# Grouped attention: outputs one pair of units later, shares copied by VectorE

## Chip, cores and metric

One NeuronCore of a Trainium2 chip runs the whole program. The metric is the device time in microseconds of one execution, as the median of several runs. All engines run at once and are held together by semaphores that the program waits on. TensorE multiplies, VectorE and ScalarE work on rows, GpSimd does a little arithmetic and issues transfers, SyncE issues the stream of weights.

## What is computed

The reference is a two-layer block, then a second block with grouped attention, retention and a mixture of experts. The change touches only the grouped attention of the second block:

```python
def one_block(q_blk):        # 128 queries; 8 query heads, 2 key/value heads, 64 features each
    s = jnp.einsum('bqhgd,bkhd->bhgqk', q_blk, k).astype(jnp.float32) * scale
    p = jax.nn.softmax(s, axis=-1)
    return jnp.einsum('bhgqk,bkhd->bqhgd', p.astype(v.dtype), v)
```

There are 512 queries (`LT` = 4 tiles of 128) and 768 keys (`NT` = 6 tiles of 128: 256 of the context and 512 latent). So there are 4 x 8 = 32 units (`S_UNITS`), each one query tile of one head, with 128 x 768 scores.

## The kernel before

**Units and pairs.** Units are done in pairs u, u+1 (u even). The two units of a pair belong to the two key/value heads, and lie in the two halves of the partitions for the scores' inputs and for the outputs. A unit goes through four jobs: scores `S` (three passes of products, high and low parts, 128 x 768), row maximum and exponential, transposes `T` of the six 128 x 128 pieces, and outputs `O`.

**PSUM slots.** PSUM is cut into four slots of two banks (1024 float32 columns). A job takes a slot: `begin` waits until the job before it in that slot was evacuated (`s_ev`), `end` tells that it is filled (`s_mm`). `filled` and `evacuated` are the waits for these, `own(...)` issues an instruction and has its engine wait for its end, `own.free(...)` issues it without. The slots and the order of all jobs are written by `make_plan`; `attention_jobs` gives the grouped attention's: `S` of unit n in slot n % 2, `T` and `O` of unit n in slot 2 + n % 2. TensorE walks the jobs in exactly this order.

**TensorE per pair (lines 2386 to 2405).** Transposes of u, transposes of u+1, scores of u+2 and u+3, then a job `O` u with the shares and a job `O` u+1 with the outputs. The shares: VectorE writes `share`, the identity scaled by the reciprocal sum of each row; a product with ones turns it into a PSUM tile in which each column holds the reciprocal of its query, laid out as the transposed outputs are. After u = 24 comes the modulation product `ada(2, 8)` in slot 2, after the loop `ada(2, 9)`, then the retention products (line 2427).

**ScalarE per pair (lines 1121 to 1138).** Copies of both units' transposes from PSUM into `ptg`; `out_high` of the pair before (the high part of `o_f` into `xth`); copy of the shares from PSUM into `shares`; exponentials of u+2 and u+3 (line 1005), which also sum the rows and free the scores' slots. After u = 6 it makes the exponential of `near`, the powers of the retention decay.

**VectorE per pair (lines 1760 to 1782).** Row maxima of u+2 and u+3 (line 1512); `out_low` of the pair before (line 1754); the outputs times `shares` into `o_f` (line 1769), which frees the outputs' slot; `sharing(u + 2)`, the reciprocal and two scaled identities (lines 1743, 1747); then a piece of other work: in pairs 4 to 7 two low parts of weights (line 1228), from pair 8 two sums of a modulation chunk (line 1275; the first of a chunk is line 1273). In pair 1 it writes `near` (lines 1562 to 1565), after pair 12 it adds the bias of `ada(2, 8)` (line 1288).

**SyncE** streams the weights through three buffers `raw` (line 628). The second half of modulation chunk 9 goes into the buffer that chunk 8 leaves, so its transfer waits for the product `ada(2, 8)`; VectorE needs it at its first sum of pair 14.

Of the kernel before, what the change touches and what calls it, by code (L numbers as in the profile page):

```python
# [16 lines left out]
P = 128  # L17
# [105 lines left out]
def make_plan(src):  # L123
# [123 lines left out]
    attention_jobs(plan, "gqa", range(S_UNITS), (24, lambda: plan.job("ada", 2, 8, slot=2)))  # L247
# [30 lines left out]
def build(nc, src, out):  # L278
# [8 lines left out]
    with ExitStack() as stack:  # L287
# [17 lines left out]
        sb("gate_region", [P, 2 * KB])  # L305

# [99 lines left out]
        sin_t = sb("sin_t", [P, SEQ])  # L406
        vecs = sb("vecs", [P, VECS])
# [3 lines left out]
        tmp = sb("tmp", [P, 2, TOK])  # L411
# [426 lines left out]
        def _(act):  # L838
# [275 lines left out]
            def out_high(u):  # L1114

                m, h = gqa_unit(u)
                evacuated(act, "O", "gqa", u + 1)
# [99 lines left out]
        def _(dve):  # L1217
# [339 lines left out]
            def near_powers():  # L1557

                d = dist[:, R_ZERO:R_ZERO + P]
                back = tmp[:, 1, 0:R_HEADS * P].rearrange("p (h n) -> p h n", h=R_HEADS)  # L1560
                for h in range(R_HEADS):
                    own.free(nc.vector.tensor_scalar(near[:, h, :], d, 0.0, lg[:, h:h + 1], ALU.max, ALU.mult))
                    own.free(nc.vector.tensor_scalar(back[:, h, :], d, 0.0, lgt[:, h:h + 1], ALU.min, ALU.mult))
                own.wait()
                own(nc.vector.tensor_tensor(near[:], near[:], back, ALU.add), s_arg)
# [172 lines left out]
            def sharing(u):  # L1738
# [5 lines left out]
                if u >= 2:  # L1744
                    filled(dve, "O", "gqa", u - 2)
                for n in range(2):
                    own.free(nc.vector.tensor_scalar(share[:, n, :], ident[:], st[:, n, 3:4], None, ALU.mult), s_share)

            def out_low(u):
# [5 lines left out]
                                                 ALU.subtract), s_ol)  # L1755

# [3 lines left out]
            for i in range(S_UNITS // 2):  # L1760
# [979 lines left out]
```

## Time and profile before

| | |
|---|---|
| runs shown (3) | median 1795.95 us, 1794.54 to 1797.14 |
| the profiled execution | 1800.47 us, its span 1798.8 us |
| busy over the span | TensorE 88%, VectorE 51%, ScalarE 30%, GpSimd 10% |
| grouped attention | 1012 to 1112.75 us |
| chain that ended last | TensorE 56%, transfers 16%, VectorE 16%, ScalarE 4% |

The profile is of one execution, by its hardware records. The busy windows give each engine's busy time and TensorE's granted clock in a stretch (1.00 is 2.4 GHz, 0.50 is 1.2 GHz). The chain of waits goes back from the last instruction to what released each one. The timeline lists instructions in order of time, equal ones merged. "Issue" is time in which an engine waited for nothing that the profile shows. Matmuls are pipelined, so a group's busy time overlaps its neighbours'.

### The profile page before, as it was taken

What the parts mean: (1) busy time and instruction counts of PE and PEld (TensorE: products, weight loads), DVE (VectorE), ACT (ScalarE), POOL (GpSimd) and SP (SyncE); (2) the same over time, 40 slices, a digit from 0 to 9 for tenths busy, and PEclk for the clock granted to TensorE, in tenths of its full rate; (3) what the DMA queues carried; (4) which work ended last, traced back from release to release, by engine and by line L of the source; (5) the groups of instructions that cost most, each with busy time, mean ns of one, the idle gap of its engine ahead of it and who ended that gap; (6) DMA issues with size and microseconds to landing.
All of it is one profiled execution on the core that took longest, in us unless ns stands there. A gap on an engine that the chain in (4) does not pass through costs nothing.

```text
span 1798.8 us, 22831 instructions
## 1 busy us (share of the span) xinstructions
PE 1587.1 (88%) x8464; PEld 1131.5 (63%) x8464; DVE 911.0 (51%) x1578; ACT 539.1 (30%) x859; POOL 181.2 (10%) x263
## 2 busy tenths in 40 slices
PE   6699999799799989998999888796999898989880
PEld 6588888688688868787788677676434333333330
DVE  3876537567458656576597876764121111111115
ACT  3312222467233354443523475122111110101011
POOL 2000010023110100001201300110000000000002
PEclk9899999769899999999999899895999999999995
DMA  9232354100332310223444012226999999999984
GB/s 371 73 115 94 137 192 169 53 13 20 115 126 89 136 49 36 105 72 140 160 177 150 1 48 95 103 90 250 366 423 423 423 423 422 423 423 423 423 355 146
DMA packets 55795, 353.07 MB, mean 196 GB/s; under 512 B 7408, under 2 KB 7664, under 8 KB 18720
## 3 DMA queue, kind: packets, MB, share of 16 engines
q1 hardware_dynamic: 43056, 306.88, 42.6%
q0 software_dynamic: 12656, 45.07, 6.8%
q8 instruction: 53, 0.87, 0.2%
q14 instruction: 30, 0.25, 0.0%
HBM read 332.26 MB, written 23.59 MB: 198 GB/s over the span
## 4 chain that ended last, share of the span: by engine, by line
PE 56%; DMA 16%; DVE 16%; ACT 4%; issue 3%; SPq 3%; POOL 0%; DVEq 0%; POOLq 0%; ACTq 0%
PE ps L2081 10%; DMA early<-in_experts 10%; PE ps L2083 10%; PE ps L2082 10%; PE ps L2563 6%; PE ps L2135 3%; DMA raw<-in_experts 3%; PE ps L2584 3%; PE ps L2267 3%; SPq L640 2%; PE ps L2544 2%; PE ps L2291 2%; PE ps L2060 1%; PE ps L2284 1%; DMA early<-in_ada 1%
## 5 line engine op out<-in xcount | busy, mean ns | idle before, releaser
L2081 PE MATMUL ps<-whi,xth 128*128 128x512 f32 (+1 forms) x768 | 305.7, 398 | 12.6 <-DVE xtl L1623 5.4
L2082 PE MATMUL ps<-wlo,xth 128*128 128x512 f32 (+1 forms) x768 | 302.0, 393 | 0.0
L2083 PE MATMUL ps<-whi,xtl 128*128 128x512 f32 (+1 forms) x768 | 301.6, 393 | 0.0
L1981 DVE TENSOR_TENSOR hid<-hid,ps 128x256 f32<-128x256 f32 x33 | 13.9, 422 | 370.4 <-ACT hid L1179 370.4
L2081 PEld LDWEIGHTS ps<-whi,xth 128*128 128x128 f32 x768 | 148.4, 193 | 43.0 <-DVE xtl L1623 5.7
L2083 PEld LDWEIGHTS ps<-whi,xtl 128*128 128x128 f32 x768 | 148.0, 193 | 30.3
L2082 PEld LDWEIGHTS ps<-wlo,xth 128*128 128x128 f32 x768 | 148.5, 193 | 28.9
L2563 PE MATMUL ps<-early,xe_t 128*64 128x512 f32 x624 | 142.3, 596 | 13.9 <-DMA early<-in_experts 12.9
L1228 DVE TENSOR_TENSOR wlo<-raw,whi 128x2048 fp32r<-128x2048 f32 (+3 forms) x52 | 103.1, 1984 | 70.6 <-ACT whi L850 64.4
L850 ACT ACTIVATE whi<-raw 128x2048 fp32r<-128x2048 f32 (+2 forms) x46 | 85.5, 1858 | 123.1 <-DMA raw<-in_even 33.5
L2563 PE MATMUL ps<-raw,xe_t 128*64 128x512 f32 x432 | 101.1, 600 | 19.1 <-DMA raw<-in_experts 16.1
L2563 PEld LDWEIGHTS ps<-early,xe_t 128*64 128x64 f32 x624 | 43.1, 137 | 109.4 <-issue 74.1
L1275 DVE SCALAR_TENSOR_TENSOR raw<-raw,cvec 128x512 f32<-128x512 f32 x140 | 105.2, 752 | 4.8
L2584 PE MATMUL ps<-early,hid_t 128*64 128x512 f32 x408 | 94.9, 601 | 1.7 <-DVE hid_t L1985 0.5
L1512 DVE TENSOR_REDUCE stat<-ps 128x1 f32<-128x768 f32 x64 | 61.3, 957 | 62.1 <-PE ps L2284 50.3
L1179 ACT ACTIVATE hid<-ps 128x256 f32<-128x256 f32 x33 | 12.7, 384 | 253.9 <-PE ps L2563 253.9
L2563 PEld LDWEIGHTS ps<-raw,xe_t 128*64 128x64 f32 x432 | 28.1, 136 | 89.2 <-issue 45.1
L818 POOL DMA_DIRECT2D pair_dram<-tmp x66 | 34.5, 523 | 471.3 <-ACT tmp L1184 468.2
L2544 PE MATMUL ps<-h2h,hot 128*128 128x512 f32 x144 | 61.2, 425 | 6.1 <-DVE hot L1969 6.1
L667 POOL TENSOR_SCALAR stat<-stat 128x1 f32<-128x1 f32 (+3 forms) x36 | 12.0, 334 | 533.5 <-ACT xtl_f L949 156.7
L1184 ACT ACTIVATE tmp<-ps 128x512 f32<-128x512 f32 x33 | 19.7, 597 | 136.8 <-PE ps L2584 136.8
L2584 PEld LDWEIGHTS ps<-early,hid_t 128*64 128x64 f32 x408 | 26.4, 136 | 51.0 <-issue 45.5
(438 smaller groups left out, 2829.5 us busy)
## 6 DMA issues: line engine op xcount, KB each, us to landing
early<-in_experts SPq DMA_DIRECT2D x129, 1024.0 KB, 26.1
raw<-in_experts SPq DMA_DIRECT2D x54, 1024.0 KB, 26.1
raw<-in_ada SPq DMA_DIRECT2D x40, 1024.0 KB, 6.6
ring<-in_experts SPq DMA_DIRECT2D x15, 1024.0 KB, 27.7
raw<-in_even SPq DMA_DIRECT2D x14, 1024.0 KB, 5.2
raw<-in_second SPq DMA_DIRECT2D x10, 1024.0 KB, 5.4
pair_dram<-tmp POOLq DMA_DIRECT2D x66, 128.0 KB, 5.8
early<-in_ada SPq DMA_DIRECT2D x8, 1024.0 KB, 18.4
```

Of the source, the lines that this page charges most:

```text
L850: own(nc.scalar.activation(whi[:, k % SPLIT, 0:w], raw[:, number[splits[k]["name"]] % RAW, 0:w], ACT.Copy), s_hi)
L1228: own(nc.vector.tensor_tensor(wlo[:, k % SPLIT, at_], raw[:, g % RAW, at_], whi[:, k % SPLIT, at_].bitcast(F32), ALU.subtract), s_lo if pa ...
L1275: ins = nc.vector.scalar_tensor_tensor(dst, w[kt // 4][:, kt % 4, :], cv, dst, ALU.mult, ALU.add)
L1512: own(nc.vector.tensor_reduce(st[:, 1:2], v[:, 0:TOK], AX, ALU.max, negate=True), nb)
L2081: nc.tensor.matmul(v, a[0], b[0], start=first, stop=False)
L2082: nc.tensor.matmul(v, a[0], b[1], start=False, stop=False)
L2083: return nc.tensor.matmul(v, a[1], b[0], start=False, stop=last)
L2135: mm = nc.tensor.transpose(v[:, to:to + P], rows_, ident[:])
L2267: mm = nc.tensor.matmul(v[:, TOK:TOK + n], pts[w % 2][:, P * a:P * a + P], v_of(w, a), start=a == 0, stop=a == NT - 1)
L2544: mm = nc.tensor.matmul(ps[:, h, :], hot[:, m, :], part[:, m, 512 * h:512 * h + 512], start=m == 0 and part is h2h, stop=m == LT - 1 and p ...
L2563: mm = nc.tensor.matmul(ps[SLOT * t:SLOT * t + SLOT, 4 + s, :], xe_t[:, 2 * i + k, SLOT * s:SLOT * s + SLOT], w[:, D * k + 512 * t:D * k + ...
L2584: mm = nc.tensor.matmul(ps[SLOT * t:SLOT * t + SLOT, 7, :], hid_t[:, s, P * c + SLOT * k:P * c + SLOT * k + SLOT], w[:, D * k + 512 * t:D ...
```

## The change

- **Order.** TensorE runs T(u), S(u+2) and S(u+3), O(u-2), T(u+1). The outputs of a pair come one pair later, between the scores of the next pair and the transposes of the second unit. The last outputs follow the loop.
- **One job for the outputs.** Shares and outputs of a pair are one job `O` u in slot 2 (columns 896 to 1023 and 768 to 895). `T` of even units stays in slot 2, of odd ones in slot 3.
- **Shares by VectorE.** `out_shared` copies the shares from PSUM into `r_f` on VectorE, waits for itself, and multiplies. ScalarE's copy is gone. `out_high` and `out_low` run two pairs late instead of one. In VectorE's round `sharing` now stands after the weights' parts.
- **Buffers.** `ptg` and `share` are doubled; the second `ptg` is `tmp`. `near` moves into free halves of `cos_t` and `sin_t`, in two pieces, so its exponential is two instructions.
- **Modulation chunk 8.** Its product comes after u = 26 instead of 24, in slot 3 instead of 2; VectorE adds its bias in pair 13 instead of 12.

```diff
--- before.py
+++ after.py
@@ make_plan
-    attention_jobs(plan, "gqa", range(S_UNITS), (24, lambda: plan.job("ada", 2, 8, slot=2)))
+    for u in range(2):
+        plan.job("S", "gqa", u, slot=u)
+    for u in range(0, S_UNITS + 2, 2):
+        if u < S_UNITS:
+            plan.job("T", "gqa", u, slot=2)
+            for n in (u + 2, u + 3):
+                if n < S_UNITS:
+                    plan.job("S", "gqa", n, slot=n % 2)
+            if u:
+                plan.job("O", "gqa", u - 2, slot=2)
+            plan.job("T", "gqa", u + 1, slot=3)
+        else:
+            plan.job("O", "gqa", u - 2, slot=2)
+        if u == 26:
+            plan.job("ada", 2, 8, slot=3)
+    plan.next = 0
...
@@ buffers
-        near = at("near", xt_base, 20 * KB, [P, R_HEADS, P])
-        share = at("share", xt_base, 45 * KB, [P, 2, P])
-        shares = at("shares", xt_base, 46 * KB, [P, 2, P])
-        ptg = at("ptg", g_base, 0, [P, 2, TOK])
+        share = at("share", xt_base, 45 * KB, [P, 2, 2, P])
+        r_f = at("r_f", xt_base, 21 * KB, [P, P])
+        ptg = [at("ptg0", g_base, 0, [P, 2, TOK]), tmp]
+        near = [t[:, SEQ // 2:SEQ].rearrange("p (h n) -> p h n", h=2) for t in (cos_t, sin_t)]
...
@@ ScalarE
+            def keys_first(n):
+                v = filled(act, "T", "gqa", n)
+                if n >= 4:
+                    filled(act, "O", "gqa", n // 2 * 2 - 4)
+                own.free(nc.scalar.activation(ptg[n // 2 % 2][:, n % 2, :], v[:, 0:TOK], ACT.Copy), ev("T", "gqa", n))
+
             for u in range(0, S_UNITS, 2):
-                for n in (u, u + 1):
-                    v = filled(act, "T", "gqa", n)
-                    if u >= 2:
-                        filled(act, "O", "gqa", u - 1)
-                    own.free(nc.scalar.activation(ptg[:, n % 2, :], v[:, 0:TOK], ACT.Copy), ev("T", "gqa", n))
-                if u >= 2:
-                    out_high(u - 2)
-                v = filled(act, "O", "gqa", u)
+                keys_first(u)
                 if u >= 4:
-                    evacuated(act, "O", "gqa", u - 3)
-                own.free(nc.scalar.activation(shares[:, u // 2 % 2, :], v[:, TOK:TOK + P], ACT.Copy), ev("O", "gqa", u))
+                    out_high(u - 4)
                 if u + 2 < S_UNITS:
                     exps("gqa", u + 2, pg, s_nbg)
                     exps("gqa", u + 3, pg, s_nbg)
+                keys_first(u + 1)
                 if u == 6:
                     act.wait_ge(s_arg, 3)
-                    own.free(nc.scalar.activation(near[:], near[:], ACT.Exp), s_fade)
+                    for j in range(2):
+                        own.free(nc.scalar.activation(near[j], near[j], ACT.Exp), s_fade)
+            out_high(S_UNITS - 4)
             out_high(S_UNITS - 2)
...
@@ VectorE
-                if u >= 2:
-                    filled(dve, "O", "gqa", u - 2)
+                if u >= 4:
+                    filled(dve, "O", "gqa", u - 4)
...
+            def out_shared(u):
+
+                v = filled(dve, "O", "gqa", u)
+                own(nc.vector.tensor_copy(r_f[:], v[:, TOK + P:TOK + 2 * P]))
+                own(nc.vector.tensor_tensor(o_f[:, u // 2 % 2, :], v[:, TOK:TOK + P], r_f[:], ALU.mult), ev("O", "gqa", u))
...
                 if i:
-                    out_low(u - 2)
-                v = filled(dve, "O", "gqa", u + 1)
-                evacuated(dve, "O", "gqa", u)
-                own(nc.vector.tensor_tensor(o_f[:, i % 2, :], v[:, TOK:TOK + P], shares[:, i % 2, :], ALU.mult),
-                    ev("O", "gqa", u + 1))
-                if u + 2 < S_UNITS:
-                    sharing(u + 2)
+                    out_shared(u - 2)
+                if i >= 2:
+                    out_low(u - 4)
                 if 4 <= i < 8:
                     for n in range(2):
                         low_part(("sout", "o", (i - 4) // 2), 2 * (i % 2) + n, 4)
                 elif i >= 8:
                     for n in range(2):
                         add_part(2, 8 + (i - 8) // 4, 2 * (i % 4) + n)
+                if u + 2 < S_UNITS:
+                    sharing(u + 2)
                 if i == 1:
                     near_powers()
-                if i == 12:
+                if i == 13:
                     ada(2, 8)
+            out_low(S_UNITS - 4)
+            out_shared(S_UNITS - 2)
             out_low(S_UNITS - 2)
...
@@ TensorE
+            def gqa_turn(w):
+                evacuated(pe, "S", "gqa", w)
+                turn(("T", "gqa", w), [pg[:, w % 3, P * a:P * a + P] for a in range(NT)], [P * a for a in range(NT)])
+
+            def gqa_out(u):
                 v = begin("O", "gqa", u)
                 pe.wait_ge(s_share, u + 2)
...
+                evacuated(pe, "T", "gqa", u + 1)
                 for a in range(NT):
...
+            gqa_scores(0)
+            for u in range(0, S_UNITS, 2):
+                gqa_turn(u)
+                if u + 2 < S_UNITS:
+                    gqa_scores(u + 2)
+                if u:
+                    gqa_out(u - 2)
+                gqa_turn(u + 1)
+                if u == 26:
                     ada(2, 8)
+            gqa_out(S_UNITS - 2)
```

## Rows read from the trace of the kernel before

**Rows 1.** Busy windows: the stretch, its length, each engine's busy time, clock, transfers

```profile
core 0: us, PE busy (x) PEld busy (x) DVE busy (x) ACT busy (x) POOL busy (x), PEclk, DMA share, GB/s
...
1066.00:1071.30 5.30, 4.66 (x53) 3.78 (x52) 4.33 (x10) 4.05 (x8) 0.00 (x0) 1.00 0.57 184
...
1095.60:1101.80 6.20, 6.08 (x53) 4.98 (x52) 3.05 (x8) 4.17 (x9) 0.00 (x0) 0.73 0.39 161
...
1012.00:1112.75 100.75, 81.97 (x846) 66.93 (x845) 74.18 (x147) 65.03 (x129) 15.61 (x8) 0.92 0.12 43
...
1112.75:1115.75 3.00, 3.00 (x29) 3.00 (x30) 0.16 (x1) 0.00 (x0) 0.00 (x0) 0.50 0.54 175
```

**Rows 2.** Chain of waits, one steady pair: start, duration, engine and what it wrote

```profile
1066.06 1.27 PE ps L2381 x11
...
1068.47 0.95 ACT pg L1005 x2
1069.53 0.73 issue
```

**Rows 3.** Chain of waits: the row maxima that begin pairs 2, 12, 13 and 14

```profile
1035.64 0.97 DVE stat L1512
...
1088.76 0.97 DVE stat L1512
...
1097.96 0.97 DVE stat L1512
...
1103.30 0.97 DVE stat L1512
```

**Rows 4.** Timeline around the modulation product of chunk 8: start, duration, instruction, wait

```profile
1090.24 1.05 PE L2060 MATMUL ps<-half,raw 128*128 128x1 f32 x8
...
1093.83 0.16 DVE L1288 TENSOR_TENSOR mod<-ps,vecs 128x4 f32<-128x4 f32 x1
1094.11 1.29 PEld L2135 LDWEIGHTS ps<-ident,pg 128*128 128x128 f32 x12 [2.90 <-issue]
```

**Rows 5.** Timeline at the stage's end: the modulation product of chunk 9

```profile
1111.74 1.08 PE L2060 MATMUL ps<-half,raw 128*128 128x1 f32 x8 [2.06 <-DVE raw L1275]
```

**Rows 6.** Waits of the transfer queue from 1205 us: total, times, longest

```profile
SPq L640 <- PE ps L2563: 59.8, 12, 48.1
```

**Rows 7.** Timeline of one steady pair: TensorE, and ScalarE's copy of transposes

```profile
1065.18 0.87 PE L2135 MATMUL ps<-ident,pg 128*128 128x128 f32 x6
1065.99 0.50 PE L2381 MATMUL ps<-ka_h,qa_h 64*128 64x512 f32 x2
...
1067.51 1.48 PE L2401 MATMUL ps<-ptg,kk 128*64 128x128 f32 x24
...
1066.10 0.81 ACT L1126 ACTIVATE ptg<-ps 128x768 f32<-128x768 f32 x1 [0.18 <-PE ps L2135]
```

**Rows 8.** Timeline of one steady pair: VectorE

```profile
1065.26 0.17 DVE L1743 RECIPROCAL stat<-stat 128x2 f32<-128x2 f32 x1 [0.69 <-ACT pg L1005]
...
1065.86 1.41 DVE L1228 TENSOR_TENSOR wlo<-raw,whi 128x512 fp32r<-128x512 f32 x2
1067.42 1.95 DVE L1512 TENSOR_REDUCE stat<-ps 128x1 f32<-128x768 f32 x2
1069.41 0.29 DVE L1754 TENSOR_TENSOR xtl<-o_f,xth 128x128 fp32r<-128x128 f32 x1
1069.62 0.28 DVE L1769 TENSOR_TENSOR o_f<-ps,shares 128x128 f32<-128x128 f32 x1
```

**Rows 9.** VectorE's copies from PSUM elsewhere: shortest/median/longest ns, first and last start

```profile
L1985 DVE COPY hid_t<-ps x33: 423/425/425, 1269.1 to 1749.8; 128x256 f32<-128x256 f32 x33
...
L1975 DVE COPY xe_t<-ps x36: 680/691/693, 1258.0 to 1740.4; 128x512 f32<-128x512 f32 x36
```

**Rows 10.** Timeline: two modulation sums on VectorE in one pair

```profile
1081.85 1.53 DVE L1275 SCALAR_TENSOR_TENSOR raw<-raw,cvec 128x512 f32<-128x512 f32 x2
```

**Rows 11.** Timeline: the exponential of the powers on ScalarE

```profile
1043.83 0.62 ACT L1138 ACTIVATE near<-near 128x512 f32<-128x512 f32 x1
```

**Rows 12.** Timeline at the stage's start: VectorE's first shares, GpSimd's products

```profile
1016.72 6.50 DVE L1747 TENSOR_SCALAR share<-ident,stat 128x128 f32<-128x128 f32 x2
...
1018.61 4.52 POOL L789 TENSOR_TENSOR gr_b<-gr,gn 128x2048 f32<-128x2048 f32 x1
```

**Rows 13.** Transfer issues from 1090.5 to 1091.6: size, us from issue to landing

```profile
raw<-in_ada SPq DMA_DIRECT2D x1, 1024.0 KB, 4.9
```

More of the change, by code:

```diff
@@ L305, in build @@
         sb("gate_region", [P, 2 * KB])
+        tmp = sb("tmp", [P, 2, TOK])
         def at(name, base, offset, shape, dt=F32):
@@ L369, in build @@
         rk_t = at("rk_t", xt_base, 12 * KB, [P, 2, 2, SEQ])
-        near = at("near", xt_base, 20 * KB, [P, R_HEADS, P])
+        near_back = at("near_back", xt_base, 20 * KB, [P, 2, P])
         pg = at("pg", xt_base, 36 * KB, [P, 3, TOK])
-        share = at("share", xt_base, 45 * KB, [P, 2, P])
-        shares = at("shares", xt_base, 46 * KB, [P, 2, P])
+        share = at("share", xt_base, 45 * KB, [P, 2, 2, P])
         o_f = at("o_f", xt_base, 47 * KB, [P, 2, P])
-        ptg = at("ptg", g_base, 0, [P, 2, TOK])
+        r_f = at("r_f", xt_base, 21 * KB, [P, P])
+        ptg = [at("ptg0", g_base, 0, [P, 2, TOK]), tmp]
         qw_t = at("qw_t", xt_base, 36 * KB, [P, R_HEADS, SEQ])
@@ L1559, in near_powers @@
                 d = dist[:, R_ZERO:R_ZERO + P]
[L1560 to L1565, printed above, removed]
+                for j in range(2):
+                    for i in range(2):
+                        h = 2 * j + i
+                        own.free(nc.vector.tensor_scalar(near[j][:, i, :], d, 0.0, lg[:, h:h + 1], ALU.max, ALU.mult))
+                        own.free(nc.vector.tensor_scalar(near_back[:, i, :], d, 0.0, lgt[:, h:h + 1], ALU.min, ALU.mult))
+                    own.wait()
+                    own(nc.vector.tensor_tensor(near[j], near[j], near_back[:], ALU.add), s_arg if j else None)
             for i in range(2):
@@ L1743, in sharing @@
                 own(nc.vector.reciprocal(st[:, :, 3:4], st[:, :, 2:3]))
-                if u >= 2:
-                    filled(dve, "O", "gqa", u - 2)
+                if u >= 4:
+                    filled(dve, "O", "gqa", u - 4)
                 for n in range(2):
-                    own.free(nc.vector.tensor_scalar(share[:, n, :], ident[:], st[:, n, 3:4], None, ALU.mult), s_share)
+                    own.free(nc.vector.tensor_scalar(share[:, u // 2 % 2, n, :], ident[:], st[:, n, 3:4], None, ALU.mult), s_share)
             def out_low(u):
@@ L1802, in states @@
                     if n == 1:
-                        dve.wait_ge(s_fade, 3)
+                        dve.wait_ge(s_fade, 4)
                         weighted_scores(0)
@@ L1810, in weighted_scores @@
                 two = slice(2 * j, 2 * j + 2)
-                own.free(nc.vector.tensor_tensor(sw[:, two], v, near[:, two, :].unsqueeze(2).broadcast_to([P, 2, LT, P]),
+                own.free(nc.vector.tensor_tensor(sw[:, two], v, near[j].unsqueeze(2).broadcast_to([P, 2, LT, P]),
                                                  ALU.mult), ev("RS", j))
@@ L2383, in gqa_scores @@
                                 end(mm, "S", "gqa", u + i)
-            gqa_scores(0)
-            for u in range(0, S_UNITS, 2):
-                for w in (u, u + 1):
-                    evacuated(pe, "S", "gqa", w)
-                    turn(("T", "gqa", w), [pg[:, w % 3, P * a:P * a + P] for a in range(NT)], [P * a for a in range(NT)])
-                if u + 2 < S_UNITS:
-                    gqa_scores(u + 2)
+            def gqa_turn(w):
+                evacuated(pe, "S", "gqa", w)
+                turn(("T", "gqa", w), [pg[:, w % 3, P * a:P * a + P] for a in range(NT)], [P * a for a in range(NT)])
+            def gqa_out(u):
                 v = begin("O", "gqa", u)
@@ L2394, in _ @@
                 for i in range(2):
-                    mm = nc.tensor.matmul(v[halves[i], TOK:TOK + P], half[:, 1:2].broadcast_to([P, 64]), share[:, i, :],
-                                          start=True, stop=True)
-                end(mm, "O", "gqa", u)
-                v = begin("O", "gqa", u + 1)
+                    nc.tensor.matmul(v[halves[i], TOK + P:TOK + 2 * P], half[:, 1:2].broadcast_to([P, 64]),
+                                     share[:, u // 2 % 2, i, :], start=True, stop=True)
+                evacuated(pe, "T", "gqa", u + 1)
                 for a in range(NT):
@@ L2401, in _ @@
                         mm = nc.tensor.matmul(v[halves[i], TOK:TOK + P], kk[:, a, P + 64 * i:P + 64 * i + 64],
-                                              ptg[:, i, P * a:P * a + P], start=a == 0, stop=a == NT - 1)
-                end(mm, "O", "gqa", u + 1)
-                if u == 24:
+                                              ptg[u // 2 % 2][:, i, P * a:P * a + P], start=a == 0, stop=a == NT - 1)
+                end(mm, "O", "gqa", u)
+            gqa_scores(0)
[7 more added lines that the diff above has]
+                if u == 26:
                     ada(2, 8)
+            gqa_out(S_UNITS - 2)
             ada(2, 9)
```

3 lines of the change are left out of this document (1 added, 2 removed).

## The prediction

> **What bounds the kernel now.** I read the busy windows first, the chain of waits next, then the timeline of one pair of units. The windows show that in the grouped attention (1012 to 1112.75 us, 100.75 us) no engine is full: TensorE 82.0 us, VectorE 74.2, ScalarE 65.0, granted clock 0.92 [rows 1]. A stage like that is set by a loop of waits. The chain of one steady pair names it: scores on TensorE, the row maximum on VectorE, the exponential on ScalarE, 0.73 us of "issue" (the second unit's exponential), then the second unit's transposes, which stand ahead of the next scores [rows 2]. Its length is the distance of the row maxima: from 1035.64 to 1088.76 there are ten pairs, 5.31 us each; in the piece used below, 5.33 [rows 3]. The next pair takes 9.20 us (1088.76 to 1097.96), because the modulation product of chunk 8 stands there, the one after 5.34, and from 1103.30 to the start of the retention products (1112.82) it is 9.52 [rows 3, 4, 5].
>
> What follows the stage is timed by its start: TensorE, ScalarE and VectorE in turn until the experts, and there the transfer queue has waited 48.1 us for TensorE [rows 6]. A microsecond won here should reach the end.
>
> **The steady pair after the change.** M is the start of the first row maximum of a pair. TensorE now runs T(u), scores of u+2 and u+3, outputs of u-2, T(u+1). The scores wait for exp(u+1) and T(u), no longer for T(u+1): 0.87 us of transposes and their hand-over leave the old loop, 5.33 - 0.9 = 4.4 us [rows 7]. But the outputs of u-2 now lie in the slot that T(u+2) needs, and they come free only when VectorE has done both maxima and then copied and multiplied. So a new loop is late next:
> - two maxima 1.95, hand-over 0.03 [rows 8]
> - the new copy 128x128 from PSUM: copies from PSUM took 0.425 at 256 columns and 0.691 at 512 [rows 9], on a line 0.29 at 128. Bounds: 0.17, the reciprocal of two columns, and 0.425. I take 0.29.
> - wait for itself 0.04, product 0.28 [rows 8], hand-over to TensorE 0.12 (from the modulation's end to the next transposes, 1093.99 to 1094.11 [rows 4])
> - T(u+2) 0.81 until the scores issue, scores 1.33 to their end, 0.10 to the maximum [rows 2, 7, 8].
>
> Sum 4.95 us. VectorE's own round is the third loop: 1.98 for the maxima, 0.33 copy, 0.32 product, 0.25 for the low part, then reciprocal, shares and two weight parts 2.05 (1065.26 to 1067.27 and 0.04), which is 4.93; with two modulation sums of 1.53 instead of 1.41 it is 5.05 [rows 8, 10]. Removing ScalarE's copy of the shares (0.28) earns nothing by itself: ScalarE waits for the maximum anyway. TensorE's issue per pair is 1.62 for transposes, 1.26 scores, 1.75 outputs, some 4.5, below all of these. The outputs of u-2 need the slot's transposes copied by ScalarE: two exponentials, then two copies of 0.81 [rows 7], end 4.65 us after M, 0.1 us before TensorE wants them: covered, but barely. If that cover goes, the delay goes straight into the pair.
>
> Six of the ten pairs go by 4.95, four by some 5.03 (the first sum of a chunk is cheaper): 49.8 instead of 53.1, a gain of 3.3. Once ScalarE makes the powers' exponential (0.62 before, two pieces now, some 0.75) between maxima and copies that are now on the edge [rows 11]; I charge 0.4. **Steady part: -2.9.** With the copy at its bounds it is -4.2 (VectorE's round then limits the last pairs) or -1.4.
>
> **The start.** The first shares take 6.50 us because VectorE sits behind GpSimd's product that ends at 1023.1 [rows 12]. The change leaves that order alone, so max(2) starts at about 1023.1 in both. Then T(2) need not wait for the first outputs, but TensorE has stood idle 2 us longer and issues it and the scores at 1.2 GHz; the powers on VectorE follow later in its round. I get max(6) at 1035.2 instead of 1035.64: **-0.4**, bounds 0 and -2.
>
> **The modulation product.** Before, chunk 8 shares slot 2 with the next transposes: they wait for TensorE's 1.05 us product and for VectorE, which first does shares and two sums (1093.83) [rows 4]. After, it comes after T(27) in slot 3, while T(28) uses slot 2. The pair from M(26) to M(28) becomes an ordinary one, 5.03 instead of 9.20: **-4.2**. The next pays: the product waits until ScalarE has copied T(27), which stands behind exp(28) and exp(29). T(27) is done 3.7 us after the scores of 28 begin, the copy 5.3, the product runs to 6.4, T(28) to 7.2, scores and hand-over 1.43: M(30) is 7.2 after M(28) instead of 5.34: **+1.9**. Before, the clock fell in this place, 0.73 over the next pair [rows 1], and the scores took 0.95 longer. The idle time is 1.5 us now against 2.8; I charge half of it: **+0.5**.
>
> The half chunk of weights that the queue loads behind this product is needed by VectorE at its sum in pair 14. Before, a whole pair lay between; now 5.2 us. It landed in 4.9 [rows 13]: no wait, with 0.2 to spare. Bounds 0 and 2 us.
>
> **The end.** Without scores the last outputs are strung out: O(28) needs T(30) copied, O(30) needs O(28) multiplied and T(31) copied, and only then comes the product of chunk 9. From M(30): out_shared(26) ends 2.6, T(30) 3.5, its copy 4.7, O(28) 6.5, T(31) 7.3, its copy 8.1, O(30) 9.5, product 10.6, against 9.5 before, where the product waited 2.06 for VectorE's sums [rows 5]: **+1.1**.
>
> **Sum:** -2.9 - 0.4 - 4.2 + 1.9 + 0.5 + 1.1 = -4.0 us. The profiled execution was 1800.47 (span 1798.8 and 1.7 around it), so 1796.5; the shown runs have the median 1795.95, 4.5 lower, so 1791.9. What can be told from no change here is about 0.2%, 3.6 us: the forecast lies just beyond it.
>
> **Rivals.**
> (a) VectorE takes the steady gain back. For: it is at 4.3 of 5.3 us in a pair [rows 1], and the loop now runs through it twice over. If copy and hand-overs cost 0.4 more per pair, the steady part is near 0 and the whole -1.1: 1794.8. Against: its rows are regular to 0.01 us. Chance 0.22, within 0.2%.
> (b) The clock holds. After chunk 9 the retention products ran 3.0 us at 0.50, TensorE having waited 2.06 just before [rows 1, 5]; now it waits less there. At 2.4 GHz they save 1.5, and the 0.5 charged above goes: 1789.9. Chance 0.2, faster.
> (c) The clock falls, the other side. Transposes, scores and outputs are now separated by waits on two engines, and one fall costs more since TensorE's 4.5 us of issue become some 8.5 at 1.2 GHz, against a pair of 5.0: 3.5 us for each pair run so. Two pairs wipe out the gain, from the third it is slower by over 0.2%; with three, 1791.9 + 10.5 = 1802.4. Against: in steady pairs the clock is 1.00 with two waits of 0.35 to 0.5 us each time [rows 1], and the change fills part of them. Chance 0.13, slower.
> The Trainium skill, "TensorE: Matmul & The Clock Gate", section "A second HAM failure mode: psum-queue depth-cycling", says that frequent micro-idles between groups of matmuls can make the clock oscillate. By that rule (c) would be the normal case and the kernel already in it; this trace doesn't agree in the steady pairs, so I leave (c) at its small chance.
>
> **How the numbers follow.** Forecast 0.45 (its own range -2.5 to -5.5, of which 0.3 lies beyond 3.6 us), (a) 0.22, (b) 0.2, (c) 0.13. Faster 0.3 + 0.2 + 0.02 = 0.52, same 0.33, slower 0.15 (some of (a) if the weights land late as well). The range runs from (b), with the better bound of the copy, 1788, to 1798, where (a) is joined by a late landing.
>
> **What would show it.** Right: row maxima 4.95 us apart in the first steady pairs and 5.05 with modulation sums; T(u+2) released by the product into o_f, no longer by the exponential; max(26) to max(28) ordinary, the next pair over 7 us with TensorE idle before the modulation product and ScalarE named; the last outputs waiting for ScalarE's copies. Wrong: pairs of 5.3 or more with VectorE busy throughout; TensorE waiting for the copied transposes in each pair; a granted clock under 1.00 in the steady windows; a landing that VectorE waits for in pair 14.

## The result and the profile after

| | before | after |
|---|---|---|
| median of the runs taken together | 1796.55 us (1794.54 to 1797.94) | 1784.18 us (1782.3 to 1785.85) |
| ratio, 95% interval | | 0.9933 [0.9916, 0.995] |
| the same two programs once more | 1794.22 us (16 runs) | 1788.51 us (11 runs) |
| ratio, 95% interval | | 0.9964 [0.9949, 0.9978] |
| profiled execution, span | 1800.47, 1798.8 us | 1785.85, 1784.1 us |
| grouped attention, first scores to retention products | 101.6 us | 94.4 us |

The changed kernel is faster. The forecast was -4.0 us and 1791.9, its range 1788 to 1798. The first comparison gave -12.4 and 1784.18, below the range; the second, of the same two programs, gave -5.7 and 1788.51, inside it. So the two comparisons differ by 6.7 us with nothing changed in the programs, and the first can't be explained to its end by the change. Over the runs of both (15 of after, mean 1787.2, and 20 of before, mean 1795.2) the change is worth about -8 us.

The busy windows of the kernel after, read as in [rows 1]: a steady pair, the pair behind the modulation product, the first 3 us of the retention products, the whole stage.

```profile
core 0: us, PE busy (x) PEld busy (x) DVE busy (x) ACT busy (x) POOL busy (x), PEclk, DMA share, GB/s
1062.00:1067.00 5.00, 4.70 (x58) 3.89 (x56) 4.70 (x11) 3.59 (x7) 0.00 (x0) 1.00 0.61 213
1086.62:1093.54 6.92, 5.58 (x64) 4.73 (x66) 4.92 (x11) 3.69 (x7) 0.00 (x0) 1.00 0.18 34
1104.00:1107.00 3.00, 3.00 (x51) 2.83 (x51) 0.36 (x2) 0.17 (x2) 0.00 (x0) 1.00 0.63 194
1009.50:1104.00 94.50, 79.57 (x850) 65.16 (x851) 81.20 (x163) 58.59 (x114) 16.49 (x8) 0.95 0.13 46
```

Before, the retention products began at a clock of 0.50 and did 29 matmuls in 3 us [rows 1]; now it is 1.00 and 51. In the stage VectorE is busier (81.2 of 94.5 us against 74.2 of 100.75), and it got shorter all the same.

The chain of waits of one steady pair after. It goes from one maximum to the next over TensorE, and the exponential and its "issue" of [rows 2] are no longer in it:

```profile
1062.84 0.97 DVE stat L1530
1063.84 0.30 DVE r_f L1779
1064.16 0.30 DVE o_f L1780
1064.46 0.14 issue
1064.60 0.85 PE ps L2160 x6
1065.44 1.27 PE ps L2406 x11
1066.74 0.97 DVE stat L1530
```

The chain in a pair with two modulation sums. Here it stays on VectorE, from sums to reciprocal and shares, and on to the next maximum. That is the commoner picture: of the ten pairs from 1032.48 to 1081.76 the chain crosses over TensorE's transposes and scores in two, in one it runs through ScalarE's copies and the powers, and in the others it ends along VectorE's own round.

```profile
1069.67 0.67 DVE raw L1293
1070.36 0.77 DVE raw L1293
1071.15 0.18 DVE stat L1762
1071.35 0.32 DVE share L1766 x2
```

The timeline after at the marks of [rows 3], the maxima that begin pairs 2, 12, 13 and 14, with those of pairs 3 and 4 beside them, then the product of chunk 8 with what it waited for.

```profile
1032.48 1.95 DVE L1530 TENSOR_REDUCE stat<-ps 128x1 f32<-128x768 f32 x2
1037.36 1.95 DVE L1530 TENSOR_REDUCE stat<-ps 128x1 f32<-128x768 f32 x2 [0.80 <-PE ps L2406]
1042.22 1.95 DVE L1530 TENSOR_REDUCE stat<-ps 128x1 f32<-128x768 f32 x2 [1.05 <-PE ps L2406]
...
1081.76 1.94 DVE L1530 TENSOR_REDUCE stat<-ps 128x1 f32<-128x768 f32 x2
...
1086.62 1.95 DVE L1530 TENSOR_REDUCE stat<-ps 128x1 f32<-128x768 f32 x2
1090.41 1.05 PE L2085 MATMUL ps<-half,raw 128*128 128x1 f32 x8 [1.34 <-ACT tmp L1142]
1093.54 1.95 DVE L1530 TENSOR_REDUCE stat<-ps 128x1 f32<-128x768 f32 x2 [1.75 <-PE ps L2406]
```

The timeline after at the stage's end, against [rows 5]:

```profile
1098.03 0.44 PE L2418 MATMUL ps<-share,half 128*64 128x128 f32 x4 [0.90 <-ACT tmp L1142]
...
1101.49 1.53 PE L2423 MATMUL ps<-tmp,kk 128*64 128x128 f32 x24 [0.53 <-ACT tmp L1142]
1102.95 1.05 PE L2085 MATMUL ps<-half,raw 128*128 128x1 f32 x8
```

The last outputs wait for ScalarE, as forecast, but by 0.90 and 0.53 us; the product of chunk 9, before which TensorE stood 2.06 us, waits for nothing.

In pairs 2 and 3, in which VectorE has no other work, it waits 0.80 and 1.05 us for the scores, and they take 4.88 and 4.86. From 1047.22 to 1081.76 it waits for nothing.

Where the time went, from the two profiles. Max(n) is the first row maximum of units n and n+1; RU is the start of the retention products; "the experts" is the first product that reads the experts' weights from `early` (5.2 us behind the very first one). The chain puts RU 0.07 us later than the timeline, hence 101.7 and 94.5 here.

| piece | before | after | difference | forecast |
|---|---|---|---|---|
| first scores to max(6) | 24.54 | 22.98 | -1.56 | -0.4 |
| ten pairs | 53.12 | 49.28 | -3.84 | -2.9 |
| max(26) to max(28) | 9.20 | 4.86 | -4.34 | -4.2 |
| max(28) to max(30) | 5.34 | 6.92 | +1.58 | +1.9, and +0.5 for the clock |
| max(30) to RU | 9.52 | 10.47 | +0.95 | +1.1 |
| the stage (sum of the above) | 101.7 | 94.5 | -7.2 | -4.0 |
| RU to the experts | 152.1 | 146.4 | -5.7 | 0 |
| experts to the end | 533.9 | 533.8 | -0.1 | 0 |

Ahead of the stage, where the programs are the same, the profile of after is 1.6 us shorter, which is chance. The profiled execution before was itself 4.5 us above the median of the runs shown.

### The profile page after: what moved, and what is told of

Same layout as the page of the kernel before. It is cut to its first block, busy times and chain, and to the rows that moved or that the text cites. A ratio compares the mean times of both kernels' runs of the same rounds, so it can differ in the third digit from the quotient of the medians.

```text
span 1784.1 us, 22804 instructions
## 1 busy us (share of the span) xinstructions
PE 1573.7 (88%) x8464; PEld 1119.4 (63%) x8464; DVE 918.4 (51%) x1595; ACT 532.5 (30%) x844; POOL 180.7 (10%) x263
## 4 chain that ended last, share of the span: by engine, by line
PE 56%; DMA 17%; DVE 16%; ACT 4%; issue 3%; SPq 3%; POOL 0%; DVEq 0%; POOLq 0%; ACTq 0%
PE ps L2106 10%; DMA early<-in_experts 10%; PE ps L2108 10%; PE ps L2107 10%; PE ps L2595 6%; PE ps L2160 3%; DMA raw<-in_experts 3%; PE ps L2616 3%; PE ps L2292 3%; SPq L657 2%; PE ps L2576 2%; PE ps L2316 2%; PE ps L2085 2%; DVE stat L1530 1%; ACT p L938 1%
## 5 line engine op out<-in xcount | busy, mean ns | idle before, releaser
L2108 PEld LDWEIGHTS ps<-whi,xtl 128*128 128x128 f32 x768 | 147.0, 191 | 30.3
L2616 PE MATMUL ps<-early,hid_t 128*64 128x512 f32 x408 | 94.8, 601 | 1.7 <-DVE hid_t L2010 0.5
```

The lines of the kernel that those rows point to most:

```text
L2108: return nc.tensor.matmul(v, a[1], b[0], start=False, stop=last)
L2616: mm = nc.tensor.matmul(ps[SLOT * t:SLOT * t + SLOT, 7, :], hid_t[:, s, P * c + SLOT * k:P * c + SLOT * k + SLOT], w[:, D * k + 512 * t:D ...
```

## Experiments: what limits a steady pair

Theory A is the prediction's: the pair is the loop from the maxima over the shares' copy, the product, T(u+2) and the scores. Its rival B: VectorE is full, whatever it does first. Both give a pair near 4.9, so the copy was doubled in one kernel and moved to ScalarE in another. Expected of the shares copied twice:

> The changed kernel with VectorE's copy of the shares made twice, one after the other, each with its wait. Theory A: 0.33 us more in each of the 13 pairs after the first two maxima and about 0.3 at the end, so 4.5 us slower than the changed kernel, 1788.7, pairs of 5.2 and 5.33. Rival B gives the same. Rival C (the copy has cover and the gain is the clock's): under 1 us slower.

```diff
                 own(nc.vector.tensor_copy(r_f[:], v[:, TOK + P:TOK + 2 * P]))
+                own(nc.vector.tensor_copy(r_f[:], v[:, TOK + P:TOK + 2 * P]))
```

Expected of the copy made by ScalarE behind both exponentials:

> The changed kernel, but ScalarE copies the shares, after its two exponentials. Theory A (the pair is the loop maxima, shares' copy, product, T(u+2), scores): ScalarE is free 3.05 us after the first maximum, so the product starts at 3.4 instead of 2.3 and each pair takes 6.0 to 6.1 us instead of 4.9 to 5.0: some 14 us slower than the changed kernel, 1798, no better than before. Rival B (the pair is the sum of VectorE's work, which is full): VectorE loses 0.33 us of work per pair, so the pairs of 5.0 fall to 4.7 and the time is 2 to 4 us lower than the changed kernel, 1781.

```diff
+            def shares_copied(u):
+                v = filled(act, "O", "gqa", u)
+                own.free(nc.scalar.activation(r_f[:], v[:, TOK + P:TOK + 2 * P], ACT.Copy), s_lam1)
...
                     exps("gqa", u + 3, pg, s_nbg)
+                if u:
+                    shares_copied(u - 2)
                 keys_first(u + 1)
...
-                own(nc.vector.tensor_copy(r_f[:], v[:, TOK + P:TOK + 2 * P]))
+                dve.wait_ge(s_lam1, u // 2 + 2)
```

Copied twice: 1792.51 us, 0.9985 [0.9973, 0.9996], 4.0 above the changed kernel's second median and 8.3 above its first; 4.5 were expected. The stage is 98.5 us, 4.1 longer. Steady pairs 5.21, with sums 5.33: +0.33 and +0.32, the length of one copy with its wait. The chain of the kernel that copies twice has it in line, and its timeline shows the two pairs without other work on VectorE:

```profile
1053.72 0.30 DVE r_f L1779
1054.05 0.30 DVE r_f L1780
1054.38 0.30 DVE o_f L1781
```

```profile
1036.11 1.95 DVE L1530 TENSOR_REDUCE stat<-ps 128x1 f32<-128x768 f32 x2 [1.35 <-PE ps L2407]
1041.32 1.95 DVE L1530 TENSOR_REDUCE stat<-ps 128x1 f32<-128x768 f32 x2 [1.36 <-PE ps L2407]
```

These are pairs 2 and 3, and they take 5.22 and 5.21 as well, though VectorE waits 1.35 us for the scores in each. A full VectorE can't explain that; the loop does.

Copied by ScalarE: 1803.43 us, 1.0041 [1.0028, 1.0054], slower than the kernel before (1798 was expected). Pairs are 5.9 to 6.1. Its chain shows the second unit's exponential (line 1022) leading to the copy and on to the product, and its timeline what VectorE waited before that product.

```profile
1061.97 0.19 ACT pg L1022
1062.16 0.18 ACT r_f L1147
1062.46 0.30 DVE o_f L1788
```

```profile
1062.46 0.29 DVE L1788 TENSOR_TENSOR o_f<-ps,r_f 128x128 f32<-128x128 f32 x1 [1.39 <-ACT r_f L1147]
```

VectorE does less per pair here and waits 1.39 us, and the pair is 1.0 longer. So what counts here is how soon behind the maxima the outputs' slot comes free, and B as the sole cause falls. But A is not the sole cause either. The loop sets pairs 2 and 3, in which VectorE waits for the scores. With two weight parts VectorE's own round fills 4.88 us without a wait, as long as the loop, and with two sums it is the longer one (5.01). A shorter loop alone would gain little in these pairs; no run has tried it.

## Experiments: the modulation product

The product put back where it was, in the changed kernel:

> The changed kernel with chunk 8's modulation product put back after u = 24 and into slot 2, its bias back in pair 12. Theory A (the stage's gain is the sum of its waits: the new loop's pairs and the moved product): the pairs before 12 stay at 4.9 to 5.0 us; T(26) waits again for VectorE's bias, which now stands after sums and shares, so max(26) to max(28) becomes 8 to 9 us instead of 4.86, while max(28) to max(30) falls from 6.92 to 5.0: 1.5 to 2.5 us slower than the changed kernel, about 1786.5. If the granted clock falls in that wait, another 1. Rival C (most of the 12 us came with the moved product, through the clock that it kept up): at least 5 us slower than the changed kernel, 1789 or more, with a low granted clock after the product.

```diff
-        if u == 26:
-            plan.job("ada", 2, 8, slot=3)
+        if u == 24:
+            plan.job("ada", 2, 8, slot=2)
... (and the same in TensorE's loop; VectorE: i == 13 becomes i == 12)
```

It took 1789.13 us, 0.9959 [0.9947, 0.9971]; 1786.5 was expected by A, 1789 or more with a low clock behind the product by rival C. The stage is 96.4 against 94.4. The two pairs there are 8.68 and 5.01 instead of 4.86 and 6.92. Its timeline shows T(28) behind VectorE's bias, as in [rows 4], and the maximum 3.79 us late:

```profile
1081.43 1.05 PE L2085 MATMUL ps<-half,raw 128*128 128x1 f32 x8 [0.34 <-DVE o_f L1780]
...
1083.53 0.15 DVE L1306 TENSOR_TENSOR mod<-ps,vecs 128x4 f32<-128x4 f32 x1
1083.83 1.32 PE L2160 MATMUL ps<-ident,pg 128*128 128x128 f32 x6 [1.34 <-DVE mod L1306]
...
1087.47 1.95 DVE L1530 TENSOR_REDUCE stat<-ps 128x1 f32<-128x768 f32 x2 [3.79 <-PE ps L2406]
```

The clock was low behind the product, 0.51 from 1084.00 to 1087.50, and RU to the experts took 150.6 us, 4.2 more than after. So both signs of rival C came out, and the time can't decide: the changed kernel itself gave 1784.18 and 1788.51. The stage can: the product's place is worth 2.0 us of it, clock included, and the other pairs stay at 4.87 to 5.01. Most of the stage's gain did not come with the moved product; whether the 4.2 us behind the stage did is open.

The move by itself, in the kernel before:

> The kernel before with one part of the change alone: chunk 8's modulation product after u = 26, slot 3, its bias in pair 13. Theory A: the order of before makes T(u+1) stand right after T(u), so T(29) waits for VectorE's bias as T(26) did: max to max 8.5 to 9 us in one pair as before, 0.8 us saved at most, about 1795.5 to 1796.5, that is no change. So the 4.3 us that this place gained came from the order and the move together. Rival C: the move alone gives 4 us or more, 1792.5 or less, with pair 12 at 5.3 and pair 13 under 7.

```diff
-    attention_jobs(plan, "gqa", range(S_UNITS), (24, lambda: plan.job("ada", 2, 8, slot=2)))
+    attention_jobs(plan, "gqa", range(S_UNITS), (26, lambda: plan.job("ada", 2, 8, slot=3)))
... (and the same in TensorE's loop; VectorE: i == 12 becomes i == 13)
```

1798.16 us, 1.001 [0.9994, 1.0026]: no gain, as expected. The pair of 9.2 only moves one on: 5.32, then 9.04. In the old order both units' transposes stand ahead of the scores; T(29) needs the slot that the product fills, and waits behind VectorE's bias, and the scores with it. In the new order T(29) comes after the scores, so the product's place is good only together with that order. This is the timeline of the move alone:

```profile
1092.27 1.05 PE L2060 MATMUL ps<-half,raw 128*128 128x1 f32 x8 [0.96 <-DVE o_f L1769]
...
1095.07 0.16 DVE L1288 TENSOR_TENSOR mod<-ps,vecs 128x4 f32<-128x4 f32 x1
1095.38 1.07 PE L2135 MATMUL ps<-ident,pg 128*128 128x128 f32 x6 [1.34 <-DVE mod L1288]
```

In all three kernels the bias stands last in VectorE's round: 2.54 us behind the product's end before [rows 4], 1.75 in the move alone, 1.05 with the product put back. So something can be had without any move. In the kernel before, the bias right behind the product into `o_f`:

> The kernel before with one line moved: VectorE adds chunk 8's bias in pair 12 right after the product into o_f, ahead of shares and sums. Theory A (the 9.2 us pair was T(26) behind VectorE's queue in slot 2): the bias ends at 1091.5 instead of 1094.0, T(26) starts 2.4 us earlier and max(26) to max(28) is 6.7 us; stage 2.4 us shorter, about 97.7 to 99.3. Rival (the product itself or the clock makes the long pair): over 8.5 us still.

```diff
                     ev("O", "gqa", u + 1))
+                if i == 12:
+                    ada(2, 8)
                 if u + 2 < S_UNITS:
                     sharing(u + 2)
...
-                if i == 12:
-                    ada(2, 8)
```

1790.3 us, 0.9976 [0.9966, 0.9985]. Its timeline has the bias 0.11 us behind the product and the transposes 0.15 behind that; the pair fell from 9.20 to 5.80, more than to the 6.7 expected, and the stage is 97.8 us (97.7 to 99.3 expected).

```profile
1085.75 1.05 PE L2060 MATMUL ps<-half,raw 128*128 128x1 f32 x8
...
1086.91 0.16 DVE L1288 TENSOR_TENSOR mod<-ps,vecs 128x4 f32<-128x4 f32 x1 [0.17 <-PE ps L2060]
1087.22 1.50 PE L2135 MATMUL ps<-ident,pg 128*128 128x128 f32 x12 [0.42 <-DVE mod L1288]
```

The 0.9 us beyond that fit the clock. In the next section's kernel, whose program is that of before up to chunk 9, the same pair took 8.24 us, and its window shows a clock of 1.00 where [rows 1] has 0.73:

```profile
1088.20:1102.20 14.00, 10.27 (x112) 8.46 (x113) 9.01 (x20) 8.46 (x19) 0.00 (x0) 1.00 0.41 153
```

8.24 less the expected 2.4 is 5.8. So of the 9.20 in the profile before, 0.96 go with a low clock that the same order has in one profile and not in another, and as much of the -4.34 in the table above is not shown to be the move's own.

The same idea in the new order: the product ahead of T(27), the bias right behind `out_shared`.

> The changed kernel with chunk 8's product ahead of T(27) in slot 3, which is free there, and its bias right behind the product into o_f in pair 13. Theory A: TensorE no longer waits for ScalarE's copy of T(27); bias and T(27) follow the product of 1.05 us, so max(28) to max(30) is 6.0 us instead of 6.92 and the stage 93.5. If a wait for the bias takes the place of the wait for the copy: 6.9 or more.

```diff
+            if u == 26:
+                plan.job("ada", 2, 8, slot=3)
             plan.job("T", "gqa", u + 1, slot=3)
...
                     out_shared(u - 2)
+                if i == 13:
+                    ada(2, 8)
... (their old places are empty; TensorE's ada(2, 8) stands ahead of gqa_turn(u + 1))
```

max(28) to max(30) is 5.83 instead of 6.92, 1.1 us less. The stage as a whole was 94.8 us and not the expected 93.5, because the first 3 us of scores ran at a clock of 0.50 in this profile. The time, 1786.62 us, 0.9948 [0.9932, 0.9965], does not tell it from the changed kernel.

## Experiments: the clock behind the stage

The clock in the first 3 us of the retention products was 0.50, 0.72 and 0.51 in three profiles of the old order (before, the move alone, the early bias), and 1.00 in all ten of the new. What differs just ahead is TensorE's wait for VectorE's sums before chunk 9's product [rows 5], 2.06 us in each of the three and none in the ten. The old order with this wait filled by transposes of the identity:

> The kernel before with 16 transposes of the identity into an unused bank of its slot ahead of chunk 9's modulation product; they fill the 2.06 us in which TensorE waits for VectorE's sums there. What is open: the retention products' first 3 us had a granted clock of 0.50 and 0.72 in the two profiles with the old order, and 1.00 in all eight with the new one. Theory F (the clock falls because TensorE waits before chunk 9's product, and the new order took that wait away): clock 1.00 at the retention products, the first 48 of them in 2.8 us instead of 4.4, stage unchanged at 100 to 101.7, so about 1.5 us faster than the kernel before. Rival (chance, or something earlier in the stage): clock 0.5 to 0.8 there as before, no faster, up to 0.5 us slower.

```diff
                 v = begin("ada", layer, c)
+                for n in range(16 if (layer, c) == (2, 9) else 0):
+                    nc.tensor.transpose(v[:, 512:640], ident[:], ident[:])
```

Timeline and window of this kernel:

```profile
1105.17 1.97 PE L2049 MATMUL ps<-ident 128*128 128x128 f32 x16
```

```profile
1108.20:1111.20 3.00, 3.00 (x51) 2.83 (x51) 0.16 (x1) 0.08 (x1) 0.00 (x0) 1.00 0.66 180
```

The clock is 1.00, and the first 48 retention products take 2.82 us in its chain, as in the changed kernel's, against 4.36 before (4.19 and 4.46 in the two others of the old order):

```profile
1108.26 2.82 PE ps L2429 x48
```

So it is the wait that lowered the clock there, by one profile of the filled kernel, and the change removed the wait by the way. In time it gave 0.9989 [0.9979, 0.9999] with 1793.57 us, about 2 us and only just clear of noise. From RU to the experts this profile has 147.0 us against 150.5 to 152.1 in the three others of the old order; nine of the ten of the new order have 146.2 to 148.5. That points at more than the 1.54 us of these products, but more is not shown: with the product put back the clock was 1.00 at RU too and the stretch 150.6. The clock differs farther on too, 0.63 from 1132.8 to 1137.8 before against 0.96 from 1124.0 to 1129.0 after, 20 to 25 us behind RU in both, and no run changed it there alone.

## Experiments: the first pairs, and the same kernel again

The changed kernel once more, since its first comparison had left 8 us unexplained:

> The changed kernel once more, unchanged, beside the kernel before. What is open: of its 12 us only 7.3 lie in the stage (94.4 against 101.7 us from the first scores to the retention products), 1.6 before the first scores and 5.7 between the retention products and the experts, where both programs are the same. Theory A (those 7.3 us are chance states of the clock outside the stage): the stage is again 94 to 95 us, but the ratio comes to 0.9950 to 0.9970, 5.5 to 9 us. Rival D (the change itself gives the rest, the clock behind it included): the ratio is again near 0.9933 and the way to the experts again near 146.4 us.

The time, 1788.51 us and 0.9964, is what A expected; the 146.3 us from RU to the experts are what rival D expected, so neither holds whole. Its stage has the same pairs to 0.03 us and again 94.4 us. The two profiles' spans differ by 2.7 us, and 2.05 of these lie ahead of the first scores (1009.51 and 1011.56), where nothing was changed. This is its window of the whole stage:

```profile
1011.60:1106.00 94.40, 79.52 (x848) 65.15 (x848) 81.13 (x163) 58.51 (x114) 16.49 (x8) 0.95 0.13 46
```

What remains long in every profile is the start, where VectorE's first shares lie beside GpSimd's products [rows 12]. Its timeline after:

```profile
1014.13 2.97 DVE L1766 TENSOR_SCALAR share<-ident,stat 128x128 f32<-128x128 f32 x2
...
1016.98 4.54 POOL L806 TENSOR_TENSOR gr_b<-gr,gn 128x2048 f32<-128x2048 f32 x1
1020.38 5.70 DVE L1766 TENSOR_SCALAR share<-ident,stat 128x128 f32<-128x128 f32 x2
1021.49 4.51 POOL L806 TENSOR_TENSOR gr<-gr,gn 128x2048 f32<-128x2048 f32 x1
```

Each pair of shares ends just behind a GpSimd product (1017.10 behind 1016.98, where the product before `gr_b` ends, and 1026.08 behind 1026.00), and the maxima, which read PSUM, pass beside them in 1.95 us. Is it the form of VectorE's instruction? The first two pairs' shares as a product of two tensors, with the reciprocal broadcast:

> The changed kernel, but the shares of the first two pairs are written by tensor_tensor with the reciprocal broadcast, not tensor_scalar. In the traces both shares of a pair end only where one of GpSimd's products ends (2.97 and 5.70 us instead of 0.48). Theory E (tensor_scalar shares a port with GpSimd's products, tensor_tensor doesn't): each pair of shares takes 0.6 us, max(4) comes 4.2 us earlier, the decay powers still wait for GpSimd's last end, so the stage is 3 to 4.4 us shorter, 90 to 91.4. Rival (VectorE waits for GpSimd's data or is slowed in any operation): the shares still take 3 and 5.7 us and the stage stays at 94.4.

```diff
-                    own.free(nc.vector.tensor_scalar(share[:, u // 2 % 2, n, :], ident[:], st[:, n, 3:4], None, ALU.mult), s_share)
+                    to = share[:, u // 2 % 2, n, :]
+                    if u < 4:
+                        own.free(nc.vector.tensor_tensor(to, ident[:], st[:, n, 3:4].broadcast_to([P, P]), ALU.mult), s_share)
+                    else:
+                        ...
```

1787.06 us, 0.9955 [0.9937, 0.9972]: the form doesn't matter. Timeline of this kernel, the first shares held until 1019.27, where the first product ends (1019.11):

```profile
1012.70 6.57 DVE L1768 TENSOR_TENSOR share<-ident,stat 128x128 f32<-128x128 f32 x2
1014.56 4.55 POOL L806 TENSOR_TENSOR gr_b<-gr,gn 128x2048 f32<-128x2048 f32 x1
```

It was then put together with the early product of chunk 8:

> share_tt and ada_early together, to see whether they add up: the sum of both gains on the changed kernel, stage 89 to 90.5 us, some 4 to 5 us faster than the changed kernel. If the start's gain is taken back by the powers on VectorE or by a low clock, the stage is over 92.

That took 1784.9 us, 0.9941 [0.9926, 0.9957]; the stage was 93.6, over the expected 89 to 90.5, and the gain is the early product's (28 to 30 again 5.83). Then the same shares on ScalarE:

> The changed kernel, but ScalarE writes the shares of the first two pairs; tensor_tensor on VectorE was held as long as tensor_scalar. Theory E2 (any VectorE operation that reads two things or one twice as fast from SBUF waits for GpSimd's products, ScalarE does not): the shares take 0.3 us each, max(4) comes 3 to 4.5 us earlier, the powers wait for GpSimd's last end instead; from the first scores to max(6) 19 to 21 us instead of 23.0, stage 91 to 92.5. If ScalarE is held as well: 23 or more.

```diff
+            def first_shares(u):
+                act.wait_ge(s_lam0, u // 2 + 2)
+                for n in range(2):
+                    own.free(nc.scalar.activation(share[:, u // 2, n, :], ident[:], ACT.Copy, scale=soft[:, u + n, 3:4]), s_share)
... (called ahead of the loop, and in it behind keys_first(1); VectorE writes them from u = 4 on)
```

ScalarE isn't held. Timeline of this kernel; GpSimd's two products lie at 1013.48 and 1017.98, 4.5 us each:

```profile
1010.61 0.69 ACT L1148 ACTIVATE share<-ident,stat 128x128 f32<-128x128 f32 x2 [0.33 <-DVE stat L1771]
...
1016.83 0.69 ACT L1148 ACTIVATE share<-ident,stat 128x128 f32<-128x128 f32 x2
```

From the first scores to max(6) it is 19.46 us, against 22.98 to 24.81 in the profiles above, with the pair of the powers, 7.68, in it. Part was given back: in the 12 us that follow the clock was 0.86, and the first pair there took 6.00. Together with 7.50 from 28 to 30 that left a stage of 93.4 us, over the expected 91 to 92.5. The time is 1787.51 us, 0.9959 [0.9943, 0.9975], no better than the changed kernel. With the early product as well:

> share_act and the early modulation product together: the version that the runs point to. The stage is 1.1 us below share_act's, 90 to 91.5 us; against the changed kernel 3 to 4.5 us faster, ratio to the kernel before about 0.994 to 0.9925.

1782.1 us, 0.9933 [0.9919, 0.9946], the shortest time of all kernels. Its stage is 89.9 us, 4.5 shorter than the changed kernel's:

```profile
1007.00:1096.90 89.90, 78.83 (x849) 64.83 (x849) 73.11 (x159) 59.83 (x118) 16.59 (x8) 0.95 0.14 48
```

Its interval lies below those of the second comparison of the changed kernel, but overlaps the first; that it beats the changed kernel is likely from the medians (1782.1 against 1784.18 and 1788.51) and from the stage, not proved.

## Why the prediction was wrong in size, and which step failed

**The steady pair.** The new loop is the one written down, piece by piece in the chain above, and it sets the pair alone where VectorE waits for the scores. VectorE's round, written down as 4.93 beside it, came out as 4.88 too, and it ends last in most of the ten pairs; the two were called near, and are. The loop is 4.88 against 4.95: the copy took what was estimated (0.32 to the product's start in the chain), and the 0.07 lie in scores and hand-overs, 1.30 in place of 1.43. With two sums 5.01 against 5.03 to 5.05. Multiplied: ten pairs less 0.6 us. The powers' exponential cost one pair 0.12 (5.00 against 4.88), where 0.4 was charged by feel: T(u+1)'s copy had slack enough. **This term, -2.9, was -3.84.**

**The start.** -0.4 against -1.56. Where the first 3 us of scores ran at a clock of 0.50 the piece took 24.54 in the old order and 24.46 in the new (the early product's kernel); where they ran at 0.86 to 0.91 it took 23.11, 24.15 and 24.13, and 22.98 to 23.19. The means differ by 0.1 and 0.8, so the forecast stands within what was measured; the rest of the 1.56 is the clock of the first scores, which came out either way in both orders.

**Chunk 8.** The ordinary pair 26 (-4.34 for -4.2) and the long one behind it (+1.58 for +1.9) held to 0.3. The clock's +0.5 did not: TensorE waited 1.34 us before the product and the window shows 1.00. It isn't out of the world: in two other kernels of this order (the first shares by two tensors and by ScalarE) the clock was 0.88 over the 14 us that end 6 us before RU, and this pair took 7.37 and 7.50. The landing took 5.0 us and ended at 1096.5; VectorE's sum began 0.40 us behind the start of the low part, against 0.21 in the same kernel's other profile, and a wait of 1.01 us behind it took that up. That -4.34 agrees so well with -4.2 is partly luck in the profile that both start from: 0.96 of its 9.20 go with a clock that the same order does not always have.

**The end.** +0.95 for +1.1.

**The step that failed** is the sentence "What follows the stage is timed by its start", by which all that lies behind the stage stood in the sum at 0. The profiles have -5.7 us there, RU to the experts. The clock was priced only as a danger (+0.5). What the runs show in place of the 0 is the first part of that stretch: 48 products in 2.82 us for 4.36, -1.54, because TensorE no longer waits before chunk 9's product. In the prediction's own words it is rival (b): "After chunk 9 the retention products ran 3.0 us at 0.50, TensorE having waited 2.06 just before; now it waits less there. At 2.4 GHz they save 1.5". All three conditions were read off rows, and the prediction's own end term says that the outputs are strung out over that wait; so (b) followed from the forecast, and 0.2 was too little for it. Filling that wait in the old order showed the mechanism, and ten profiles of the new order have it. Its price of 1.5 was right, and it explains no more than that of the -5.7. The second failure is one of size: the steady part, -2.9 for -3.84.

Put right, the terms are -0.4 - 3.84 - 4.34 + 1.58 + 0.95 = -6.05 in the stage, -1.5 to -2 behind it: about -8, which is also what the runs of both comparisons give. The agreement is no proof, since 0.96 of the -4.34 is a clock that came out either way. The remaining 4 us of the first comparison, and the 4 us between RU and the experts beyond the faster products, are open: over the profiles this stretch has 146.2 to 152.1, mostly long where TensorE waited before chunk 9's product, but long as well in the kernel with the product put back, where it did not.

**The rivals.** (a) fell: VectorE's round is as long as the loop, but the pair still got 0.45 shorter. (c) fell: from 28 to 75 us behind the first scores the clock was 1.00 in nine of ten profiles of the new order and 0.96 in the tenth, where ScalarE copies the shares and the pairs are longest.

## What to carry to other kernels

- When a stage is a loop of hand-overs, write down the loop that is late next, and what each buffer's release waits for: here the copy put behind two exponentials made a pair 5.9 us, the same copy on the engine that came free first 4.88. Then write down each engine's own round beside it; here it was as long.
- A small job that borrows a slot costs what its evacuation is late. Look where the evacuating instruction stands in its engine's round before moving the job: moving the bias alone gave 0.9976, moving the product alone nothing.
- A pair that is compared may have been slow for another reason: look at its clock in several profiles before its whole length is booked as a gain (9.20 and 8.24 us here).
- Price what a removed wait does to TensorE's clock behind it, not only what a new one may do; and compare twice before explaining the last few tenths of a per cent.

## What the hardware did that was not expected

- A GpSimd product of two SBUF tensors (4.5 us) holds VectorE's product or scaling from SBUF to its end, 0.48 us of work becoming 2.97 to 6.57, but neither its maxima over PSUM (1.95) nor ScalarE doing the same scaling (0.69). The Trainium skill, "SBUF — State Buffer", section "🔬 SBUF: two separate sides", says that GpSimd and a VectorE instruction in a two-port mode or with two SBUF inputs share a pair of ports by an exclusive lock for a whole instruction, and that ScalarE never waits for anyone; these rows agree with both.
- TensorE's wait of 2.06 us was followed by a clock of 0.50 to 0.72 in three profiles out of three, and filled with transposes by 1.00.
- The same program gave 1781.97 to 1794.65 us in 11 runs, while its stage was 94.4 us in both its profiles. Of the 2.7 us between these two, 2.05 lie ahead of the first scores, and over all 14 profiles the first scores begin between 1006.0 and 1011.8 us, with the same program up to there; what makes that part shorter or longer was not found.
